# A wait on the row two places ahead, in front of each pair of table gathers

## The reference

```python
def one_block(hb):                      # 128 tokens at a time, 2 blocks
    ...                                 # scores, top 16 of each half key, top 16 pairs: idx (128, 8 heads, 16)
    g = jax.nn.softmax(top_s, axis=-1)
    u = u_tab[idx]                      # rows of 1024 floats
    act = jax.nn.gelu(jnp.einsum('thkd,td->thk', u, hb))
    wts = (g * act.astype(jnp.float32)).astype(hb.dtype)
    v = v_tab[idx]
    return jnp.einsum('thk,thkd->td', wts, v)
```

## Time and profile before

| | us |
|---|---|
| median of 3 runs | 2285.29 (2284.11 to 2286.78) |
| the profiled execution: span from the first to the last instruction | 2379.3 |
| busy PE / DVE / POOL / ACT | 2070.6 / 979.9 / 497.6 / 555.0 |
| first and last issue of a u gather | 386.6 and 1150.2 |

### The profile page before, as it was taken

One profiled execution on the slowest core, in us unless ns is written; L12 is line 12 of the kernel. 1 busy time (PEld: TensorE's weight loads), 2 busy tenths in 40 slices (PEclk: granted clock), 3 DMA queues, 4 the chain that ended last, 5 costly groups with the idle time before them and its releaser, 6 DMA issues.

```text
span 2379.3 us, 27257 instructions
## 1 busy us (share of the span) xinstructions
PE 2070.6 (87%) x9038; PEld 1171.1 (49%) x9039; DVE 979.9 (41%) x2276; ACT 555.0 (23%) x1027; POOL 497.6 (21%) x562
## 2 busy tenths in 40 slices
PE   8998998967658576584999989999999999999998
PEld 7867887623223232232678854444444444444443
DVE  5955555646647566473375232111111111111112
ACT  4636301212112111122214222211111111121112
POOL 0000003466666666665300000000000000000000
PEclk9999999988878787896999989999999999999999
DMA  7352586799999999998842428799999999999996
GB/s 301 142 212 80 195 356 262 277 368 344 370 380 344 366 364 353 371 345 327 345 180 107 176 97 372 301 429 429 428 428 428 430 428 428 429 429 428 428 429 280
DMA packets 111703, 784.34 MB, mean 330 GB/s; under 512 B 13056, under 2 KB 13312, under 8 KB 80160
## 3 DMA queue, kind: packets, MB, share of 16 engines
q1 hardware_dynamic: 37920, 515.18, 52.3%
q0 software_dynamic: 73728, 268.47, 29.8%
HBM read 782.55 MB, written 1.05 MB: 329 GB/s over the span
## 4 chain that ended last, share of the span: by engine, by line
PE 75%; issue 11%; DVE 5%; another core or an unknown queue 2%; ACT 2%; POOL 2%; DMA 1%; DVEq 0%; ACTq 0%; POOLq 0%; SPq 0%
PE ps L786 56%; PE ps L945 16%; PE ps L1210 1%; DVE ring L1942 1%; DVE arena L1942 1%; DMA arena<-in_peer_v,arena 1%; PE ps L918 1%; POOL ring L746 1%; POOL ring L744 1%; DMA ring<-in_peer_v,arena 1%; DVE arena L1700 0%; DVE arena L1891 0%; ACT arena L1372 0%; PE ps L1241 0%
## 5 line engine op out<-in xcount | busy, mean ns | idle before, releaser
L786 PE MATMUL ps<-ring,arena 128*64 128x512 f32 (+2 forms) x3336 | 749.5, 589 | 41.8 <-issue 41.7
L786 PEld LDWEIGHTS ps<-ring,arena 128*64 128x64 f32 (+1 forms) x3336 | 262.9, 140 | 501.5 <-issue 500.7
L945 PE MATMUL ps<-ring,arena 128*128 128x512 f32 x768 | 366.5, 635 | 156.8 <-issue 134.7
L786 PE MATMUL ps<-arena,ring 128*128 128x256 f32 (+1 forms) x2272 | 486.2, 373 | 3.8 <-DVE arena L1685 3.2
L786 PEld LDWEIGHTS ps<-arena,ring 128*128 128x128 f32 x2272 | 417.4, 189 | 65.5 <-issue 6.9
L945 PEld LDWEIGHTS ps<-ring,arena 128*128 128x128 f32 x768 | 154.9, 204 | 364.6 <-issue 340.0
L945 PE MATMUL ps<-arena 128*128 128x512 f32 (+2 forms) x600 | 211.3, 599 | 66.5 <-ACT arena L1278 50.6
L1942 DVE CUSTOM_DVE_ANT_0 ring<-ring,ps 128x1024 f32<-128x1024 f32 x192 | 228.1, 1218 | 94.8 <-DMA ring<-in_peer_v,arena 88.5
L1600 ACT COPY arena<-ps 128x512 f32<-128x512 f32 (+1 forms) x165 | 89.2, 541 | 739.6 <-PE ps L786 683.5
L2255 DVE TENSOR_TENSOR arena<-ps,arena 128x512 f32<-128x512 f32 x66 | 45.7, 692 | 438.4 <-PE ps L1210 438.4
L786 PE MATMUL ps<-arena 128*128 128x128 f32 (+4 forms) x1502 | 215.2, 298 | 11.1 <-ACT arena L1262 6.6
(11 more groups left out here) (336 smaller groups left out, 1214.5 us busy)
## 6 DMA issues: line engine op xcount, KB each, us to landing
ring<-in_w_exp SPq DMA_DIRECT2D x192, 2048.0 KB, 17.1
ring<-in_w_in SPq DMA_DIRECT2D x24, 2048.0 KB, 9.5
ring<-in_w_ada SPq DMA_DIRECT2D x12, 2048.0 KB, 8.8
ring<-in_w_out SPq DMA_DIRECT2D x4, 2048.0 KB, 8.2
ring<-in_w_peer_q SPq DMA_DIRECT2D x4, 2048.0 KB, 10.6
ring<-in_w_br_rnn SPq DMA_DIRECT2D x4, 1280.0 KB, 7.4
ring<-in_w_br_attn SPq DMA_DIRECT2D x2, 2048.0 KB, 13.9
ring<-in_peer_u,arena POOLq DMA_INDIRECT x192
```

The costliest lines, as they stand in the source:

```text
L786: return pe.matmul(o, l, r, start=start, stop=stop)
L945: return pe.matmul(o, l, r, start=start, stop=False, skip_group_check=True)
```

## The change

In front of each row's two gathers, POOL waits for one more thing: that both halves of the row two places in front of it have landed. For k of 2 and more that is `uv_full[k - 2]` of the same head, for k of 0 and 1 it is `uv_full[14]` and `uv_full[15]` of the head before. The head with g = 0 leaves the wait out for k of 0 and 1. As the choice is made when the program is written out, not when it runs, this holds for that head position in all four turns of tile 0's loop: heads 0, 2, 4 and 6 of tile 0. The wait is marked, so `per` grows by one for each such wait.

```diff
-                per = 2 * (2 + TOPK)
+                per = 2 * (2 + 2 * TOPK) - (2 if tile == 0 else 0)
...
+                            if g > 0 or k >= 2:
+                                before_it = (g - 1, k - 2 + TOPK) if k < 2 else (g, k - 2)
+                                own.mark(pool.wait_ge(uv_full[before_it[1]], i * 64 + 32 * before_it[0] + 32))
                             own.mark(pool.wait_ge(s_pv, i * (2 * TOPK) + TOPK * g + k + 2))
```

## The result

| | us |
|---|---|
| before, median of 4 runs | 2285.85 (2284.11 to 2286.78) |
| after, median of 4 runs | 2590.76 (2584.90 to 2593.06) |
| ratio after / before | 1.132 (95% interval 1.1305 to 1.1335); the two medians give 1.133 |
| forecast | 2497, range 2400 to 2535 |
| profiled execution of after: span | 2591.1 |

The direction and the mechanism were right, the size was not: +305 us in place of +212.

What follows compares the result with a forecast made beforehand. Before, POOL's issue and DMA bound the table stage at 2.55 us a row; after, two rows' flight: (6.81 + 0.1) / 2 = 3.45. 239 x (3.45 - 2.55) = +215, +1 - 3 = +213: 2498, forecast 2497 us, range 2400 to 2535.

Steps and rivals of the forecast that it cites:

- the 94 us: Excess of the profiled execution of the kernel before over its median run; placed in the table stage, rows 16 to 255.
- the rival that had them elsewhere: Excess outside rows 16 to 255, so runs have DVE's stalls too: +124 us, 2409 us; chance 0.25.
- DVE's stalls: Table stage: DVE idle without shown cause, 88.4 us before L1949; held to belong to profiling, runs issuing at 2.55 us a row.
- The flight: Table stage, a row's issue to its landing: 6.81 us, ends 6.48 (empty queue) and 7.61 (full queue).
- Wake: 0.1 us (ends 0 and 0.3): Table stage, landing of the row two ahead to POOL's next issue: 0.1 us, read from PE's start against POOL's.
- skipped waits: Rows 32, 64 and 96 and their followers leave the wait out; only the follower gains, 3 times: -3 us.
- first 16 rows: Rows before row 16 take 65 us, waiting for weights to be used up; the change moves row 16 by +1 us (0 to +4).
- behind the last issue: After the table stage everything starts from the last row, so it shifts as a whole: 0 us.
- Two rows suffice: Table stage: flight not over 5.0 us, two rows reach 2.55 us each, 2285 us; no-change rivals together 0.06.
- A shorter queue frees DVE: Table stage: the cap removes DVE's stalls, 2.924 falls to 2.55 us a row, 2196 us; chance 0.03.
- The wait passes at once: POOL's added wait meets a count already reached: no change, 2285 us; no-change rivals together 0.06.
- the high end of the period: Table stage, slowest pace used: (7.15 + 0.1) / 2 = 3.62 us a row, in place of 3.96.

Runs made afterwards that it cites:

- the second profile: The kernel before, unchanged, profiled once more: runs at 2287.66 us (ratio 0.9993), profiled execution with a span of 2287.3 us.

## Why the prediction was wrong

**What held.** The stage is bound by two rows' flight; the period is (flight + gap) / 2. DVE and PE have room. The wait instruction is free. POOL's copy at the head's start nearly fits in: at 6 of 15 heads the gap there is 1.28 to 1.49 us and not 0.94. The waits on `s_pv` no longer bind. The period of the runs before was taken as 2.55 and is 2.559; the choice to put the 94 us into rows 16 to 255 was right, against the rival that had them elsewhere and gave 2409. Its reason, that DVE's stalls belong to profiling, was not: the second profile has none. Span and median now stand together (2591.1 and 2590.76), as forecast. The flight was taken as 6.81 and is 6.63, within its ends. From its issue to the dot the v half needs 5.22 us even with only one row in flight (median of 232 rows). The fit of the Trainium skill (DMA: Bandwidth & Descriptors, section Anatomy of one DMA) gives an estimate of 3.2 us for such a gather. By the prediction's sum that would have made the change free; the measurement decides against it here.

**What failed: the step "Wake: 0.1 us (ends 0 and 0.3)".** It measures 0.94 us, three times its upper end. It was read from PE's start at 959.31 against POOL's at 959.43, as if PE's next pair began when `s_pv` was raised. Matmul ends are modelled and `s_pv` counts a product that may lie some matmuls back, so this pair of rows doesn't hold the interval. A row that did hold it stood in the same group: the copy at the head's start is waited for, as a landing is, and the gather behind it starts at 962.80 with 0.97 us of idle time in front of it. The chain of waits of that profile (start, us, what) shows the last wait passed and then 0.75 us up to the gather, as in the changed kernel:

```profile
962.02 0.03 POOLq L742
962.05 0.75 issue
962.80 0.29 POOL ring L744
```

The prediction charged this to the copy (0.88 us once in 16 rows). It was the price of any wait that POOL's sequencer really stands at before an indirect gather. With 0.97 for the wake the same sum gives (6.81 + 0.97) / 2 = 3.89 and 239 x (3.89 - 2.55) = 320, less 2: 2603 us, 12 from the result.

The difference, term by term, in us:

| term | forecast | measured | share of the miss |
|---|---|---|---|
| gap, 239 x (0.94 - 0.10) / 2 | 0.10 | 0.94 | +100 |
| flight, 239 x (6.63 - 6.81) / 2 | 6.81 | 6.63 | -22 |
| skipped waits, and the remainder of the period | -3 | in the period | +7 |
| first 16 rows | +1 | +13 | +12 |
| behind the last issue | 0 | -4 | -4 |

The sum is +93. What makes the last term is not known. The period's terms add up to 239 x (3.793 - 3.45) + 3 = 85. The first 16 rows are read against the second profile of the kernel before: 391.45 to 443.50, 52 us, while the changed kernel takes 390.59 to 456.58, 66 us. The forecast took 65 us as given from the odd execution, added 1 us (4 at most) and so found almost no loss. In the good one, rows 0 to 12 go at 2.49 us and only row 13 waits, for a weight buffer. In the changed kernel row 13 is already 6.8 us later (440.89 against 434.10), with the window's slower pace behind it. Then row 15 is the one held up by a weight buffer, 5.87 us idle, and it is issued at 452.21 where the good execution had it at 439.42. That later dots delay PE's last scoring jobs, and with them that buffer, is argued from the code and not tested.

**The rivals.** "Two rows suffice" falls with a flight of 6.63 us in the changed kernel, 6.16 at the least. "A shorter queue frees DVE" falls too: the second profile has a full queue and no stalls, so there was nothing to free. "The wait passes at once" is out.

**The range** failed with the same step: the high end of the period, 3.62, combined a flight of 7.15, longer than the measured one, with a wake of 0.1. With the wake's own end of 0.3 and the flight of 7.61 the prediction had 3.96 in hand, and set it aside because a full queue can't be kept up at that pace. That was right for the flight and hid that the wake had the wider error.

## What to carry to other kernels

A limit on what is in flight turns a throughput into (latency + turnaround) / depth, and both parts need a row of their own from the trace. Take the turnaround from a place where the issuing engine really stood at a wait and then did the same kind of instruction; back-to-back spacing (0.30 us here) hides it. Give a queue one entry more than latency / pace says: here 4 rows cost nothing, 3 cost 2.1%, 2 cost 13.2%, 1 cost 53%.

## What was not expected of the hardware

- Between the last wait that POOL's sequencer passes and the recorded start of an indirect gather lie 0.76 to 0.77 us; another wait with a register read in between adds 0.17 us. Back to back the gathers stand only 0.30 us apart, and POOL can do two small memsets in that time for nothing.
- The flight grows slowly with the load: 6.47, 6.63 and 7.27 us with one, two and three rows allowed in flight, against 9.47 us (146 rows) in the second profile of the kernel before, where up to 16 are.
- Gathers of 8 KB pieces, one for each row, move 421 to 422 GB/s in the stage; pairs of gathers of 4 KB pieces 409 to 410.
- One profiled execution was 92 us longer than the next of the same program. Where a span lies well above the median of the runs, its idle times must not be taken for those of the runs.
